# Gate groups moved between the halves of an expert chunk, one-hot matrices built two groups ahead

## What is computed

```
u_sel = take(u, eidx);  a = gelu(u_sel . x);  w = softmax(top scores) * a
out = sum over the chosen experts of w * v[eidx]
```

## Time and profile before

| | |
|---|---|
| time, median of 3 runs | 2904.64 us (2901.78 to 2905.84) |
| time of the profiled execution | 2905.82 us |
| its span | 2904.0 us |
| PE busy | 2544.8 us, 88% of the span |
| DVE busy | 1726.8 us, 59% |
| ACT busy | 1336.2 us, 46% |
| POOL busy | 674.4 us, 23% |
| mean granted clock of PE | 0.918 |

### The profile page before, as it was taken

One profiled execution on the slowest core, in us unless ns is written; L12 is line 12 of the kernel. 1 busy time (PEld: TensorE's weight loads), 2 busy tenths in 40 slices (PEclk: granted clock), 3 DMA queues, 4 the chain that ended last, 5 costly groups with the idle time before them and its releaser, 6 DMA issues. The chain is left out here.

```text
span 2904.0 us, 56663 instructions
## 1 busy us (share of the span) xinstructions
PE 2544.8 (88%) x16279; PEld 2319.1 (80%) x16279; DVE 1726.8 (59%) x3769; ACT 1336.2 (46%) x2336; POOL 674.4 (23%) x508
## 2 busy tenths in 40 slices
PE   6778999889999998868999889999997968786997
PEld 6678999889888887768999889888886837786995
DVE  3447777666777774446777666777775434313126
ACT  2334545556555553324445556555553312332442
POOL 4243443000000003344443000000002400443664
PEclk9589999999999998579999999999998975897999
DMA  5033555334566665023555334466664430331443
GB/s 199 1 116 129 214 200 213 127 127 159 183 240 237 246 239 197 16 87 127 209 207 208 142 126 149 178 237 241 246 237 151 177 116 5 119 123 65 168 172 130
DMA packets 94499, 469.28 MB, mean 162 GB/s; under 512 B 11473, under 2 KB 11985, under 8 KB 47185
## 3 DMA queue, kind: packets, MB, share of 16 engines
q1 hardware_dynamic: 93440, 465.57, 44.5%
q0 software_dynamic: 416, 1.57, 0.2%
q10 hardware_dynamic: 560, 1.19, 0.1%
HBM read 434.74 MB, written 33.55 MB: 161 GB/s over the span
## 5 line engine op out<-in xcount | busy, mean ns | idle before, releaser
L897 ACT ACTIVATE wh<-ring 128x512 fp32r<-128x512 f32 x1428 | 889.1, 628 | 682.6 <-ACTq L896 681.8
L1251 DVE TENSOR_TENSOR wl<-ring,wh 128x512 fp32r<-128x512 f32 x981 | 701.4, 717 | 479.9 <-DVEq L1250 462.2
L705 PE MATMUL PS<-xh,wh 128*128 128x256 f32 x2048 | 592.8, 289 | 35.6 <-PEq L701 35.5
L705 PE MATMUL PS<-xl,wh 128*128 128x256 f32 x2048 | 583.1, 285 | 0.0
L705 PE MATMUL PS<-xh,wl 128*128 128x256 f32 x2048 | 582.8, 285 | 0.0
L425 POOL TENSOR_TENSOR wl<-ring,wh 128x512 fp32r<-128x512 f32 x303 | 407.3, 1358 | 330.1 <-POOLq L424 319.6
L576 PE MATMUL PS<-wh,xh 128*128 128x512 f32 x1112 | 435.1, 391 | 7.5 <-PEq L573 7.5
L705 PEld LDWEIGHTS PS<-xh,wh 128*128 128x128 f32 x2048 | 396.9, 194 | 46.0 <-issue 45.4
L576 PE MATMUL PS<-wh,xl 128*128 128x512 f32 x1112 | 433.2, 390 | 0.0
L576 PE MATMUL PS<-wl,xh 128*128 128x512 f32 x1112 | 433.1, 390 | 0.0
L705 PEld LDWEIGHTS PS<-xl,wh 128*128 128x128 f32 x2048 | 396.8, 194 | 0.0
(11 more groups left out here) (235 smaller groups left out, 3637.0 us busy)
## 6 DMA issues: line engine op xcount, KB each, us to landing
ring<-in_peer_u SPq DMA_DIRECT2D x128, 1024.0 KB, 4.8
ring<-in_peer_v SPq DMA_DIRECT2D x128, 1024.0 KB, 4.8
acts<-stg SPq DMA_DIRECT2D x124, 256.0 KB, 2.1
gains<-acts SPq DMA_DIRECT2D x124, 256.0 KB, 4.8
ring<-in_w_in SPq DMA_DIRECT2D x24, 1024.0 KB, 4.8
ring<-in_w_gate_up SPq DMA_DIRECT2D x22, 1024.0 KB, 4.8
ring<-in_peer_wq SPq DMA_DIRECT2D x16, 1024.0 KB, 4.8
ring<-in_w_down SPq DMA_DIRECT2D x11, 1024.0 KB, 4.8
```

The lines of the kernel that those rows point to most:

```text
L705: last = pe.matmul(PS[:, 2 * j, 0:S], w[:, q, k * P:(k + 1) * P], x[:, at, :], start=at + i == 0, stop=at + i == 9)
L897: act.activation(wh[:, q, :], ring[:, s, q * QW:(q + 1) * QW], ACT.Copy).then_inc(high_ready[q], 1)
L1251: part = dve.tensor_tensor(wl[:, q, :], ring[:, s, q * QW:(q + 1) * QW], wh[:, q, :].bitcast(F32), SUB)
```

## The change

PE no longer does its gate groups behind a whole chunk. With three groups they come behind quarter 1, behind quarter 2 and behind quarter 3; with two, behind quarter 1 and behind quarter 3. ACT's copies stand between its high parts accordingly, each behind the high part after the group's half. DVE builds the one-hots of the first two groups ahead of the loops, and inside them those of the group two later than the one that PE takes in the same place.

```
 PE   def experts(beside=()):
          ...
              if q % 2 == 0:
                  last.then_inc(parts_free[q], 1)
+                 if j and len(beside) > 2:
+                     gates(beside[1])
          last.then_inc(act_full[j], 1)
+         if beside:
+             gates(beside[-j])
...
-     for k in range(2):
-         experts()
-         for m in range(3):
-             gates((3 * k + m) % 2)
+     experts((0, 1, 0))
+     experts((1, 0, 1))
  with pe.Fori(0, 14):
-     experts()
-     for m in range(2):
-         gates(m)
+     experts((0, 1))

 ACT  def experts(c, s, first=False, kept=False, at=None, slots=()):
      high(s, 0)
      expert(c - 1, 1 - s, 0, first)
      high(s, 1)
+     if slots:
+         gates_out(at, slots[0])
      high(s, 2)
+     if len(slots) > 2:
+         gates_out(at + 4, slots[1])
      expert(c - 1, 1 - s, 1, kept=kept)
      high(s, 3)
+     if slots:
+         gates_out(at + 4 * len(slots) - 4, slots[-1])
...
-     expert(NPAIR - 1, 1, 0)
-     expert(NPAIR - 1, 1, 1, kept=True)
-     for m in range(2):
-         gates_out(S - 8 + 4 * m, m)
+     for j in range(2):
+         expert(NPAIR - 1, 1, j, kept=True)
+         gates_out(S - 8 + 4 * j, j)

 DVE
+ def lows(s, at, slots):
+     low(s, 0, 2)
+     low(s, 1, 2)
+     onehots(at, slots[0])
+     low(s, 2, 2)
+     if len(slots) > 2:
+         onehots(at + 4, slots[1])
+     low(s, 3, 2)
+     onehots(at + 4 * len(slots) - 4, slots[-1])
+ for s in (0, 1):
+     onehots(4 * s, s)
...
-         for m in range(3):
-             low(1 - k, m, 2)
-             onehots(24 * i + 12 * k + 4 * m, (3 * k + m) % 2)
-         low(1 - k, 3, 2)
+         lows(1 - k, 24 * i + 12 * k + 8, (k, 1 - k, k))
...
-         for m in range(2):
-             low(1 - k, m, 2)
-             onehots(16 * i + 8 * k + 144 + 4 * m, m)
-         low(1 - k, 2, 2)
-         low(1 - k, 3, 2)
+         lows(1 - k, 16 * i + 8 * k + 152, (0, 1))
```

More of the change, by code:

```diff
@@ L693, in _, with experts @@
                 pe.sem_inc(keys_in, -16)
-                def experts():
+                def experts(beside=()):
                     for j in range(2):
@@ L1034, in expert, with experts @@
                         act.sem_inc(acts_kept[s] if kept else acts_out[s], 1)
-                def experts(c, s, first=False, kept=False):
+                def experts(c, s, first=False, kept=False, at=None, slots=()):
                     high(s, 0)
@@ L1068, in _ @@
                     for k in range(2):
-                        experts(2 * i + N_GATE + 1 + k, 1 - k)
-                        for m in range(3):
-                            gates_out(24 * i + 12 * k + 4 * m, (3 * k + m) % 2)
+                        experts(2 * i + N_GATE + 1 + k, 1 - k, at=24 * i + 12 * k, slots=(k, 1 - k, k))
                 with act.Fori(0, 6) as i:
                     for k in range(2):
-                        experts(2 * i + N_GATE + 13 + k, 1 - k)
-                        for m in range(2):
-                            gates_out(16 * i + 8 * k + 144 + 4 * m, m)
-                experts(NPAIR - 1, 1, kept=True)
-                for m in range(2):
-                    gates_out(S - 16 + 4 * m, m)
-                expert(NPAIR - 1, 1, 0)
-                expert(NPAIR - 1, 1, 1, kept=True)
-                for m in range(2):
-                    gates_out(S - 8 + 4 * m, m)
+                        experts(2 * i + N_GATE + 13 + k, 1 - k, at=16 * i + 8 * k + 144, slots=(0, 1))
+                experts(NPAIR - 1, 1, kept=True, at=S - 16, slots=(0, 1))
+                for j in range(2):
+                    expert(NPAIR - 1, 1, j, kept=True)
+                    gates_out(S - 8 + 4 * j, j)
                 act.drain().then_inc(gates_done, 1)
@@ L1556, in _ @@
                     dve.sem_inc(oneh_used[s], 1)
+                def lows(s, at, slots):
[9 more added lines that the diff above has]
+                    onehots(4 * s, s)
                 with dve.Fori(0, 6) as i:
                     for k in range(2):
-                        for m in range(3):
-                            low(1 - k, m, 2)
-                            onehots(24 * i + 12 * k + 4 * m, (3 * k + m) % 2)
-                        low(1 - k, 3, 2)
+                        lows(1 - k, 24 * i + 12 * k + 8, (k, 1 - k, k))
                 with dve.Fori(0, 6) as i:
                     for k in range(2):
-                        for m in range(2):
-                            low(1 - k, m, 2)
-                            onehots(16 * i + 8 * k + 144 + 4 * m, m)
-                        low(1 - k, 2, 2)
-                        low(1 - k, 3, 2)
[L1570 to L1576, removed]
+                        lows(1 - k, 16 * i + 8 * k + 152, (0, 1))
+                lows(1, S - 8, (0, 1))
                 for s in (0, 1):
```

## The result

The changed kernel took 2828.72 us (median of 4 runs, 2822.69 to 2836.1) beside 2904.75 of the kernel before; ratio 0.9746 (95% interval 0.9728 to 0.9765). The profiled execution was the slowest of the four, 2836.1 us, span 2834.3.

A forecast was written before the change was run, and what follows sets the result against it. Engines taking turns, none full, bound the kernel; with PE never waiting, three-group chunks gain 23.6 us, two-group 8.05, start 0.6, end -0.1: 32.15 a layer, 64.3 in two, forecast 2841 us, range 2835 to 2855.

The forecast's parts named there:

- costs 0 in my sum: In the chunks beside gate groups, ACT, DVE and their waits never hold PE up; smallest slack 0.7 us, cost 0.
- (1): The half clock stays in the gate-group stretches and at each start: 2848 to 2851 us; chance 0.07 in full.
- (d): Each layer's first chunk: one-hots before the first low part gain 0.6 us; 0 if the stall brings back half clock.
- (2): In three-group chunks one-hots come too late and the last group still stalls: +19, 2861 us; chance 0.07 with mixtures.
- (3): Waits for PE's groups in ACT's and DVE's queues hold up high and low parts: +53, 2958 us; chance 0.03.
- (a): PE's unstalled chunk: matmuls 5.83 us, groups 0.895 each, 0.08 per added passage back to experts; 8.68 with three groups, 7.70 with two.
- The 0.88 of the earlier trace: Time from a chunk's last gate group (551.95) to the next chunk (552.83), taken to agree with 0.90 us a group.
- may not be paid: Lower bound: the 0.08 us passage from group back to experts costs nothing in mid-chunk, 70 times, -6 us, giving 2835.
- to 1 us: Sign expected in the profile after: the stages before and behind the changed stretch keep their length to 1 us.

The follow-up runs named there:

- the moved copy: Against the changed kernel, ACT copies a chunk's first group ahead of high part 1 instead of behind it; 2857.46 us, ratio 0.9836 to the kernel before.
- lighter experts: Against the changed kernel, the product of high weights and low tokens is left out beside the gate groups; 2788.56 us, ratio 0.9584 to the kernel before.

## Why the prediction was right and where it failed

- That the engines took turns and that PE would be the only bound ("costs 0 in my sum"): right. PE's windows are full, and doubling its groups shows up one to one. The whole gain needs the lead, the orders of PE and ACT, and in them the copy behind the high part; the lead alone and the moved copy leave 38 and 26 us of it away. PE's order without ACT's was not run.
- Rivals: (1) the half clock went from both stretches, but in 3 of 6 layers of the changed kernel it came back behind the first group's stall, as part (d) had for its lower bound. (2) did not occur, but slack was 0.4 us, and the moved copy makes exactly this case. (3) did not occur. Its mechanism, a return path longer than a period, did not decide; what makes the same orders slow is one-hots without a lead.
- **The failed step is (a), the price of a group.** I took 8 passes at 0.112 = 0.895 and added 0.08 for each passage back to the experts. In all a group adds only the 0.895: 0.81 of it stands ahead of the next expert matmul, and the 0.08 behind that matmul is the rest. Behind a group the expert matmul is recorded 0.03 us after the last pass instead of 0.112, and its successor 0.20 later instead of 0.12: together 0.23, as 0.112 + 0.12. The passage costs nothing; I counted the late successor and not the early start. The 0.88 of the earlier trace rows that seemed to agree with 0.90 did so by luck: it belongs to a group behind a stall, which is recorded 1.13 us long where the one without a stall has 1.06, and so hid the 0.07. 64 groups x 0.085 = 5.4 us a layer, which is 216.7 - 5.4 = 211.3 against 211.19 measured with the clock full. The plain sum of spacings had it: 48 x 0.12 + 24 x 0.112 = 8.45, and 48 x 0.12 + 16 x 0.112 = 7.55. That groups side by side (7.54) and apart (7.53) come out alike confirms it.
- My bound for the same term, "may not be paid", came to -6 and gave the low end 2835. The term was off by 10.9 for two layers: the bound took back only the passages in the middle of chunks, and not the one at each chunk's end, which sits in the 5.83 of the earlier trace rows.
- The range held only doubt about the sum and none about the rest of the kernel, which I took to repeat to the microsecond. My sign of "to 1 us" for the stages before and behind failed already in the first profile (0.9, 2.1 and 1.2 us longer), and the rest differs by 16 us between profiles (2394.3 to 2410.5). With the right term the sum is 2905.8 - 75 = 2831, among the medians of the three sets (2828.7, 2831.8, 2833.0). Why the first set came out lowest of the three, no run shows.

## What to carry to other kernels

Where no engine is full, look for the turn-taking: lay out one period from the rows with who waits for whom, and put side work so that its input is ready a period early and its wait stands behind nothing urgent. Either half of such a change can be worth less or be harmful alone, as 41 us gained and 108 lost here. Price a kind of instruction by spacings over a whole run of it, from the first of one kind to the second of the next; a single interval at a change of kind misleads.

## What the runs showed of the hardware

- Plain float32 products of 128 columns are recorded here as two passes 0.112 us apart, 256-column ones of the split kind every 0.12 us. Mixing the two on PE cost nothing: groups side by side and groups between quarters gave 7.54 and 7.53 us.
- The granted clock fell behind some short stalls and not behind others of the same length. A stall of 2.84 us at the first group stands in ten layers (the changed kernel three times, the doubled groups, the moved copy), and 1.2 GHz came with it in 6; with 1.53 us there it came in none of 6, with 3.6 to 3.8 us in 3 of 4 (orders alone, lighter experts). With only the lead, PE stalled for 1.52 to 1.70 us in each of 24 chunks and the clock stayed full, while the kernel before, with 0.54 and 1.10 us a chunk, fell twice in each layer in those chunks. Stalls of 2.09 and 1.20 us in a chunk came with the full clock (12.16 us) and with a fall (13.75).
- A stretch at 1.2 GHz cost about 1.5 us where PE was needed, a longer one 2.7.
- Code that is the same instruction for instruction took 2394 to 2410 us in different executions, and one kernel's times on one chip spread over 23 us, its mean clock between 0.916 and 0.927.
